# Moving the residual add of four post-norms from VectorE to GpSimd in a two-block transformer kernel

## The chip, the cores and the metric

The kernel runs on one core of a Trainium2 chip. The time is that of one execution on the device in microseconds (us), taken by the host's measurement of the whole program; several runs give a median. One further execution is recorded by the hardware profiler, and all rows below come from it. "PE" is TensorE's matmul stream, "DVE" VectorE, "ACT" ScalarE, "POOL" GpSimd and "SP" SyncE, which only issues transfers here.

## What is computed

The program applies a "first block" and a "second block" of two layers each to a sequence of 512 tokens by 1024 features. Only the ends of the two halves of each layer in the first block matter for this change:

```
def rms_norm(x, g):
    xf = x.astype(jnp.float32)
    y = xf * lax.rsqrt(jnp.mean(xf * xf, axis=-1, keepdims=True) + RMS_EPS)
    return (y * g.astype(jnp.float32)).astype(x.dtype)

for layer in range(DEPTH):                      # first block, DEPTH = 2
    h = rms_norm(x, norm_mix_pre[layer])
    h = dilated_attention_mixer(...) if layer % 2 == 0 else rglru_mixer(...)
    x = x + rms_norm(h, norm_mix_post[layer])   # norms 1 and 3
    h = rms_norm(x, norm_ffn_pre[layer])
    h = conv_ffn(h, ...)
    x = x + rms_norm(h, norm_ffn_post[layer])   # norms 2 and 4
# second block, layer 0 begins with
h = rms_norm_2(x, mix_norm_g[layer])
proj = h @ w_in[layer]
```

So four times a mixer's or feed-forward's output is normed ("post-norm"), added to the residual `x`, and the sum is normed again ("pre-norm") for the next matrix product. The next product of norm 1 and 3 is a feed-forward, that of norm 2 the recurrent mixer, and that of norm 4 the first layer of the second block.

## The kernel before

Activations lie with the features on the partitions: `x`, `y0`, `y1`, `y2`, `h_hi` and `h_lo` are tiles of 128 partitions by 8 chunks by 512 tokens in float32, one chunk (128x512) for 128 features. Matrix products are taken to nearly full float32 accuracy by splitting each operand into a high part (rounded to the matmul's format) and a low part (the rest), and by adding three matmuls: high times high, high times low, low times high. A "unit" is one 128-wide slab of weights: SP loads it into a `raw` buffer, ACT copies it to `w_hi` (line 1353), and the low part `w_lo = raw - w_hi` is taken by GpSimd (line 631 in the attention and recurrent stages, lines 648 and 649 in halves in the second block) or, within the feed-forwards, by DVE (line 2287). PE then multiplies the unit with the eight chunks of the activations (lines 680, 681, 686 and, for the last, 683).

Each engine runs its own instruction stream in program order, with semaphores between the streams. The order is written out by hand, nothing is planned by a scheduler.

The four norms of the first block are the function `norm_pair` of the DVE stream (lines 2111 to 2125) together with `norm_pair` of the ACT stream (lines 1393 to 1398). For every chunk c:

- DVE scales the output: `y = y * gain * rstd` (line 2116, `scalar_tensor_tensor`, raises `res_mid`).
- DVE adds it to the residual: `x = x + y` (line 2120, `tensor_tensor`, raises `x_ready`), one chunk behind the scaling.
- ACT, when `x_ready` says so, writes `h_hi = x * gain` (line 1389) and the square of x into one of two `sq` buffers (line 1381).
- DVE writes `h_lo = x * gain - h_hi` (line 2102), two chunks behind the scaling.

In norms 1, 2 and 3 PE sums the squares over the features itself: `first_unit` (lines 847 to 859) waits per chunk for `h_lo` and the square, issues a matmul of ones with `sq` (line 856) and the three product matmuls of the chunk. In norm 4 (`more=False`) DVE adds up the squares in `ss` (lines 2092 and 2095, one more DVE instruction for each chunk), and PE's first unit belongs to the second block. There ACT, after its last square, loads a table of activation functions (line 2060), splits the first weight unit (line 1353), GpSimd takes its low part (lines 648 and 649), and only then PE can begin.

Of the kernel before, what the change touches and what calls it, by code (L numbers as in the profile page):

```python
# [22 lines left out]
ALU = mybir.AluOpType  # L23
# [5 lines left out]
KC = D // P  # L29
# [38 lines left out]
RING_A, RING_B = 3, 4  # L68
BANKS_A, BANKS_B = 3, 2
AHEAD = 2  # L70
RING_F, AHEAD_F = 6, 5
UNITS_ATTN, UNITS_FFN, UNITS_LRU = HEADS * 9 + KC, FF_BLOCKS * 3 * KC, 3 * KC + 4
# [182 lines left out]
def build_program(nc, t, out):  # L255

    with ExitStack() as ctx:
# [1 line left out]
            [f"raw_A{n}" for n in range(RING_A)] + [f"raw_B{n}" for n in range(RING_B)] +  # L259
            "hi_split unit_ready ffn_ready acc_full acc_freed misc_act misc_dve "  # L260
            "consts_in x_in params_in zeroed t_done x_ready cols_in f_full f_copied f_stored bias_spread bias_in "
            "h_hi h_lo sq_ready ss_ready stat_full rstd_ready res_mid "
            "hi_ready lo_ready v_turned v_hi wide_full wide_freed s_mid nmax_ready exp_done recip p_ready pt_hi pv_full "
            "o_hi o_lo conv_begun conv_mid conv_done gelu_done hid32 hid_hi hid_lo "
            "gate_done xb_ready xb_hi xb_lo lam_act lam_dve r_done a_done w_mid w_done v_done mult_done b_mid hs32 "
# [4 lines left out]
        sems = {n: ctx.enter_context(nc.semaphore(n)) for n in names}  # L270

        def sb(name, shape, dt=F32, c=ctx):
            return c.enter_context(nc.sbuf_tensor("s_" + name, shape, dt))
# [6 lines left out]
        x = sb("x", [P, KC, S])  # L280
        h_hi = sb("h_hi", [P, KC, S], F32R)
        h_lo = sb("h_lo", [P, KC, S], F32R)
        rstd = sb("rstd", [P, S])
# [64 lines left out]
        y0 = sb("y0", [P, KC, S], F32, stage)  # L348
# [3 lines left out]
        y1 = sb("y1", [P, KC, S], F32, stage)  # L352
# [6 lines left out]
        w_hi_a = w_hi + [sb(f"w_hi_f{n}", [P, KC, P], F32R, stage) for n in range(RING_F - RING_A)]  # L359
        w_lo_a = w_lo + [sb(f"w_lo_f{n}", [P, KC, P], F32R, stage) for n in range(RING_F - RING_A)]  # L360
# [11 lines left out]
        y2 = sb("y2", [P, KC, S], F32, stage)  # L372
# [250 lines left out]
        @block.gpsimd  # L623
        def _(pool):
            count = Counts(pool)

            def unit(w_hi_of, w_lo_of):

                pool.wait_ge(sems["hi_split"], count("hi_split"))
                s, w = count.slot(), count.split_slot()  # L630
                pool.tensor_tensor(w_lo_of[w][:], raw_b[s][:], w_hi_of[w][:].bitcast(F32), ALU.subtract).then_inc(sems["unit_ready"], 1)  # L631
                pool.wait_ge(sems["unit_ready"], count("unit_ready"))
                count.units += 1

            for units in (UNITS_ATTN, UNITS_LRU):
                with count.loop(units // RING_A,
                                "hi_split unit_ready") as i:
                    for _ in range(RING_A):
                        unit(w_hi_a, w_lo_a)
                for _ in range(units % RING_A):  # L640
                    unit(w_hi_a, w_lo_a)
                count.units += UNITS_FFN
                count("hi_split", UNITS_FFN)
            def unit_by_halves():

                pool.wait_ge(sems["hi_split"], count("hi_split"))
                s, h = count.slot(), KC // 2
                pool.tensor_tensor(w_lo_b[s][:, 0:h, :], raw_b[s][:, 0:h, :], w_hi_b[s][:, 0:h, :].bitcast(F32), ALU.subtract)  # L648
                pool.tensor_tensor(w_lo_b[s][:, h:, :], raw_b[s][:, h:, :], w_hi_b[s][:, h:, :].bitcast(F32),  # L649
                                   ALU.subtract).then_inc(sems["unit_ready"], 1)  # L650
                pool.wait_ge(sems["unit_ready"], count("unit_ready"))
                count.units += 1

            count.second_ring()
            with count.loop(LAYERS * UNITS_LAYER // RING_B,
                            "hi_split unit_ready") as i:
                for _ in range(RING_B):
                    unit_by_halves()
# [3 lines left out]
        def _(pe):  # L662
# [59 lines left out]
            for c in range(KC):  # L722
                if past := count("x_ready", lag=2):
                    pe.wait_ge(sems["x_ready"], past)
                turn4(bank[c % 2], [x_in[:, j, c * P:(c + 1) * P] for j in range(TT)], "t_done")

            n_dma = sum(copies * (1 + (at % P + rows - 1) // P) for at, rows, _, copies in COLS.values())
            pe.wait_ge(sems["params_in"], count("params_in", 16 * n_dma))
            if past := count("x_ready", 0):
# [612 lines left out]
        def _(act):  # L1342
# [231 lines left out]
            def sigmoids(n):  # L1574
                for dst in (r4, i4):
                    for _, b in tiles(n):
                        output(False)
                        freed()
                        fn(dst[:, b, :], dst[:, b, :], ACT.Sigmoid).then_inc(sems["r_done"], 1)
                        act.wait_ge(sems["r_done"], count("r_done"))  # L1580
# [6 lines left out]
            def decays(n):  # L1587
                nc.scalar.preload_act_table_set("natural_log_exp_and_others")
                for j, b in tiles(n):
                    fn(a4[:, b, :], r4[:, b, :], ACT.Exp, scale=lam(j)).then_inc(sems["a_done"], 1)  # L1590
                    act.wait_ge(sems["a_done"], count("a_done"))
                for _, b in tiles(n):
                    fn(r4[:, b, :], t4[:, b, :], ACT.Ln, scale=-1.0, bias=1.0).then_inc(sems["w_mid"], 1)
                    act.wait_ge(sems["w_mid"], count("w_mid"))
                for _, b in tiles(n):
                    fn(r4[:, b, :], r4[:, b, :], ACT.Exp, scale=-1.0).then_inc(sems["w_done"], 1)
                    act.wait_ge(sems["w_done"], count("w_done"))
# [479 lines left out]
        def _(dve):  # L2077
            count = Counts(dve)
            count.squares = 0
            tt, stt, ts = nc.vector.tensor_tensor, nc.vector.scalar_tensor_tensor, nc.vector.tensor_scalar  # L2080
# [18 lines left out]
            def next_lo(c, gain, add=True):  # L2099

                dve.wait_ge(sems["h_hi"], count("h_hi"))
                stt(h_lo[:, c, :], x[:, c, :], gain(c), h_hi[:, c, :].bitcast(F32), ALU.mult, ALU.subtract).then_inc(sems["h_lo"], 1)
                count("h_lo")
                if add:
                    add_square()
                else:
                    count("sq_ready")
                    count("ss_ready")
                    count.squares += 1

            def norm_pair(y, post, gain, more=True):

                dve.wait_ge(sems["rstd_ready"], count("rstd_ready"))
                for c in range(KC + 2):
                    if c < KC:
                        stt(y[:, c, :], y[:, c, :], post(c), rstd[:], ALU.mult, ALU.mult).then_inc(sems["res_mid"], 1)
                        count("res_mid")
                    if 1 <= c <= KC:
                        dve.wait_ge(sems["res_mid"], count("res_mid", 0, lag=1 if c < KC else 0))
                        tt(x[:, c - 1, :], x[:, c - 1, :], y[:, c - 1, :], ALU.add).then_inc(sems["x_ready"], 1)  # L2120
                        count("x_ready")
                    if c >= 2:
                        next_lo(c - 2, gain, not more)
                if more:
                    dve.wait_ge(sems["rstd_ready"], count("rstd_ready"))
# [176 lines left out]
            count("hi_split", UNITS_ATTN)  # L2302
            project(y0)
            norm_pair(y0, lambda c: col("norm_mix_post", c), lambda c: col("norm_ffn_pre", c))

            def ffn(layer):
# [48 lines left out]
            count.units += UNITS_LRU  # L2355
            count("hi_split", UNITS_LRU)
            norm_pair(y1, lambda c: col("norm_ffn_post", c), lambda c: col("norm_mix_pre", KC + c))

            nc.vector.memset(xpad[:, 0:LRU_CONV - 1], 0.0).then_inc(sems["zeroed"], 1)
# [115 lines left out]
            gated_lo(7)  # L2475
            project(y2)
            norm_pair(y2, lambda c: col("norm_mix_post", KC + c), lambda c: col("norm_ffn_pre", KC + c))
            ffn(1)
            norm_pair(y1, lambda c: col("norm_ffn_post", KC + c), lambda c: col("mix_norm_g_2", c), False)
# [419 lines left out]
```

## Time and profile before

| what | value |
|---|---|
| time, median of 3 runs | 3382.24 us (3378.85 to 3386.6) |
| time of the profiled execution | 3384.51 us |
| its span, first to last instruction | 3382.5 us |
| mean granted TensorE clock | 0.956 of full speed |
| PE busy | 3125.8 us (92%) |
| DVE busy | 1624.0 us (48%) |
| ACT busy | 1448.3 us (43%) |
| POOL busy | 793.0 us (23%) |

PE is busy for nine tenths of the span. The four norms are among the few places where it waits: they lie at 651.8 to 670.9 us, 1081.8 to 1100.8 us, 1289.9 to 1309.0 us and 1720.0 to 1745.5 us. GpSimd does nothing in any of the four. A row of the profile gives busy times of one group of instructions; a row of the timeline gives the start in us, the duration in us, the engine, line and operation, and in brackets how long the engine had been idle before and which instruction ended that.

### The profile page before, as it was taken

The numbers are of one execution on the slowest core, as the hardware profiler recorded it, in microseconds if no ns is written. First come the engines' busy times: TensorE is split into PE (matmuls) and PEld (weight loads), VectorE is DVE, ScalarE is ACT, GpSimd is POOL, SyncE is SP. The second block draws the span as 40 slices with busy tenths as digits, with TensorE's granted clock in tenths as the row PEclk, the third lists the DMA queues.
The fourth block names the chain that finished last, engine by engine and source line by source line (L and its number), as shares of the span: only waits on it lengthen the run. The fifth ranks groups of instructions, "written<-read, shape, count | busy, mean of one in ns | idle before, by whom it ended". The sixth has DMA issues, their size and how long they took to land.

```text
span 3382.5 us, 43848 instructions
## 1 busy us (share of the span) xinstructions
PE 3125.8 (92%) x13613; PEld 2450.7 (72%) x13613; DVE 1624.0 (48%) x2409; ACT 1448.3 (43%) x2123; POOL 793.0 (23%) x528
## 2 busy tenths in 40 slices
PE   6999999899998888999969988699998998889998
PEld 4788887678886666888847757588886775668886
DVE  4454454475665766565647454511124746341113
ACT  3333333443334565333336565433334666442223
POOL 1333323100000330000013212144443220224443
PEclk8999999899999999999979999799999998889999
DMA  8322222133331223333222111033333210213332
GB/s 197 114 75 81 79 67 73 50 112 94 94 93 56 69 75 87 99 94 94 75 81 63 50 52 51 25 95 97 94 93 95 58 58 26 63 49 95 93 93 75
DMA packets 484181, 269.42 MB, mean 80 GB/s; under 512 B 9482, under 2 KB 475474, under 8 KB 483636
## 3 DMA queue, kind: packets, MB, share of 16 engines
q1 hardware_dynamic: 477252, 255.85, 26.7%
q10 hardware_dynamic: 6768, 11.62, 1.0%
q8 instruction: 77, 1.26, 0.2%
q14 instruction: 84, 0.69, 0.1%
HBM read 264.12 MB, written 12.21 MB: 82 GB/s over the span
## 4 chain that ended last, share of the span: by engine, by line
issue 56%; PE 28%; POOL 12%; DVE 1%; ACT 1%; SPq 1%; DMA 0%; POOLq 0%; ACTq 0%; DVEq 0%
PE acc L680 8%; PE acc L681 8%; PE acc L686 7%; POOL s_w_lo L649 5%; POOL s_w_lo L648 5%; POOL s_w_lo L631 2%; PE acc L683 1%; PE wide L707 1%; PE misc L681 0%; PE misc L680 0%; PE misc L686 0%; SPq L522 0%; DMA s_raw<-attn_w_qkv 0%; DVE s_sc L2254 0%; PE wide L680 0%
## 5 line engine op out<-in xcount | busy, mean ns | idle before, releaser
L680 PE MATMUL acc<-s_h_hi,s_w_hi 128*128 128x512 f32 (+1 forms) x2064 | 855.8, 415 | 58.8 <-POOL s_w_lo L649 37.8
L681 PE MATMUL acc<-s_h_lo,s_w_hi 128*128 128x512 f32 (+1 forms) x2064 | 815.5, 395 | 0.0
L686 PE MATMUL acc<-s_h_hi,s_w_lo 128*128 128x512 f32 (+1 forms) x1806 | 713.4, 395 | 0.0
L648 POOL TENSOR_TENSOR s_w_lo<-s_raw,s_w_hi 128x512 fp32r<-128x512 f32 x208 | 268.4, 1291 | 1550.7 <-ACT s_w_hi L1353 1549.6
L1353 ACT ACTIVATE s_w_hi<-s_raw 128x1024 fp32r<-128x1024 f32 x388 | 411.4, 1060 | 387.3 <-DVE s_x L2860 210.9
L680 PEld LDWEIGHTS acc<-s_h_hi,s_w_hi 128*128 128x128 f32 x2064 | 393.3, 191 | 172.4 <-issue 68.9
L631 POOL TENSOR_TENSOR s_w_lo<-s_raw,s_w_hi 128x1024 fp32r<-128x1024 f32 x108 | 261.6, 2422 | 1010.0 <-ACT s_w_hi L1353 1007.3
L681 PEld LDWEIGHTS acc<-s_h_lo,s_w_hi 128*128 128x128 f32 x2064 | 393.6, 191 | 98.0 <-issue 15.7
L686 PEld LDWEIGHTS acc<-s_h_hi,s_w_lo 128*128 128x128 f32 x1806 | 344.2, 191 | 80.2
L680 PE MATMUL acc<-s_hid_hi,s_w_hi 128*128 128x512 f32 x752 | 297.4, 395 | 0.0
L681 PE MATMUL acc<-s_hid_lo,s_w_hi 128*128 128x512 f32 x752 | 297.3, 395 | 0.0
L649 POOL TENSOR_TENSOR s_w_lo<-s_raw,s_w_hi 128x512 fp32r<-128x512 f32 x208 | 271.4, 1305 | 0.0
L686 PE MATMUL acc<-s_hid_hi,s_w_lo 128*128 128x512 f32 x658 | 260.0, 395 | 0.0
L680 PE MATMUL acc<-s_h_hi,s_w_hi_f 128*128 128x512 f32 x432 | 176.1, 408 | 8.5 <-DVE s_w_lo_f L2287 8.5
L2850 DVE SCALAR_TENSOR_TENSOR s_u<-acc,s_rstd 128x512 f32<-128x512 f32 x64 | 44.3, 692 | 269.7 <-PE acc L683 260.4
L681 PE MATMUL acc<-s_h_lo,s_w_hi_f 128*128 128x512 f32 x432 | 172.2, 399 | 0.0
L680 PEld LDWEIGHTS acc<-s_hid_hi,s_w_hi 128*128 128x128 f32 x752 | 141.5, 188 | 33.9
L681 PEld LDWEIGHTS acc<-s_hid_lo,s_w_hi 128*128 128x128 f32 x752 | 141.5, 188 | 33.7
L1533 ACT ACTIVATE s_cv<-s_up,s_cols 128x512 f32<-128x512 f32 x96 | 78.5, 818 | 171.2 <-DVE s_up L2322 166.4
L686 PE MATMUL acc<-s_h_hi,s_w_lo_f 128*128 128x512 f32 x378 | 150.8, 399 | 0.0
L2332 DVE SCALAR_TENSOR_TENSOR s_cv<-s_up,s_cols,s_cv 128x512 f32<-128x512 f32 x192 | 144.1, 750 | 6.1
L686 PEld LDWEIGHTS acc<-s_hid_hi,s_w_lo 128*128 128x128 f32 x658 | 123.8, 188 | 29.6
(402 smaller groups left out, 4978.3 us busy)
## 6 DMA issues: line engine op xcount, KB each, us to landing
s_raw<-w_ff SPq DMA_DIRECT2D x128, 512.0 KB, 4.0
s_raw<-ffn_w_up SPq DMA_DIRECT2D x96, 512.0 KB, 3.9
s_raw<-attn_w_qkv SPq DMA_DIRECT2D x72, 512.0 KB, 3.8
s_raw<-ffn_w_down SPq DMA_DIRECT2D x48, 512.0 KB, 3.9
s_raw<-w_in SPq DMA_DIRECT2D x44, 512.0 KB, 4.1
s_raw<-lru_w_in SPq DMA_DIRECT2D x16, 512.0 KB, 3.9
s_raw<-w_out SPq DMA_DIRECT2D x16, 512.0 KB, 3.9
s_raw<-attn_w_o SPq DMA_DIRECT2D x8, 512.0 KB, 3.9
```

Of the source, the lines that this page charges most:

```text
L631: pool.tensor_tensor(w_lo_of[w][:], raw_b[s][:], w_hi_of[w][:].bitcast(F32), ALU.subtract).then_inc(sems["unit_ready"], 1)
L648: pool.tensor_tensor(w_lo_b[s][:, 0:h, :], raw_b[s][:, 0:h, :], w_hi_b[s][:, 0:h, :].bitcast(F32), ALU.subtract)
L649: pool.tensor_tensor(w_lo_b[s][:, h:, :], raw_b[s][:, h:, :], w_hi_b[s][:, h:, :].bitcast(F32), ALU.subtract).then_inc(sems["unit_ready"], 1)
L680: mm(out, ahi, bhi, start=start, stop=False, **kw)
L681: mm(out, ahi, blo, start=False, stop=False, **kw)
L683: mm(out, alo, bhi, start=False, stop=stop, **kw).then_inc(sems[sem], 1)
L686: mm(out, alo, bhi, start=False, stop=stop, **kw)
L707: nc.tensor.transpose(*args)
L1353: fn((w_hi_a if count.ring == "A" else w_hi_b)[w][:], raw_b[s][:], ACT.Copy).then_inc(sems["hi_split"], 1)
L1533: fn(cv[:, s, :], up[:, s, 2:2 + S], ACT.Identity, bias=cols[:, bass.ds(b * KC + v, 1)], scale=cols[:, bass.ds(b * KC + w, 1)]).then_inc(s ...
L2332: stt(cv[:, s, :], up[:, s, tap:tap + S], cols[:, bass.ds(b * KC + w, 1)], cv[:, s, :], ALU.mult, ALU.add).then_inc(sems[sem], 1)
L2850: stt(u2[:, n % 2, :], o[:], 0.0, rstd[:], ALU.max, ALU.mult).then_inc(sems["acc_freed"], 1)
```

## The change

The residual add leaves DVE's loop. DVE raises `post_done` after each scaling; GpSimd waits for it, adds the chunk (`x = x + y`, one `tensor_tensor` of 128x512 in float32 for each of 4 x 8 chunks) and raises `x_ready`, on which ACT goes on as before. To put the adds in their places, GpSimd's loop over weight units is cut: the adds of norm 1 follow the attention's units, the first two units of the recurrent mixer (`AHEAD` = 2, which are split before norm 2) come ahead of the adds of norm 2, and the adds of norms 3 and 4 follow the mixer's units.

```
@@ in the GpSimd stream
-            for units in (UNITS_ATTN, UNITS_LRU):
-                with count.loop(units // RING_A,
+            def residual(y):
+
+                for c in range(KC):
+                    pool.wait_ge(sems["post_done"], count("post_done"))
+                    pool.tensor_tensor(x[:, c, :], x[:, c, :], y[:, c, :], ALU.add).then_inc(sems["x_ready"], 1)
+
+            def units_of(n):
+                with count.loop(n // RING_A,
                                 "hi_split unit_ready") as i:
                     for _ in range(RING_A):
                         unit(w_hi_a, w_lo_a)
-                for _ in range(units % RING_A):
+                for _ in range(n % RING_A):
                     unit(w_hi_a, w_lo_a)
+
+            def feed_forward_units():
+
                 count.units += UNITS_FFN
                 count("hi_split", UNITS_FFN)
+            units_of(UNITS_ATTN)
+            residual(y0)
+            feed_forward_units()
+            for _ in range(AHEAD):
+                unit(w_hi_a, w_lo_a)
+            residual(y1)
+            units_of(UNITS_LRU - AHEAD)
+            residual(y2)
+            feed_forward_units()
+            residual(y1)
@@ in norm_pair of the DVE stream
                 for c in range(KC + 2):
                     if c < KC:
-                        stt(y[:, c, :], y[:, c, :], post(c), rstd[:], ALU.mult, ALU.mult).then_inc(sems["res_mid"], 1)
-                        count("res_mid")
-                    if 1 <= c <= KC:
-                        dve.wait_ge(sems["res_mid"], count("res_mid", 0, lag=1 if c < KC else 0))
-                        tt(x[:, c - 1, :], x[:, c - 1, :], y[:, c - 1, :], ALU.add).then_inc(sems["x_ready"], 1)
-                        count("x_ready")
+                        stt(y[:, c, :], y[:, c, :], post(c), rstd[:], ALU.mult, ALU.mult).then_inc(sems["post_done"], 1)
+                        count("post_done")
                     if c >= 2:
                         next_lo(c - 2, gain, not more)
```

DVE's stream before, at the start of norm 4 (`s_y` the output being scaled, `s_h_lo` the low part, `s_ss` the sum of squares; lines 2116, 2120, 2102, 2092 and 2095 as above):

```order
L2116 SCALAR_TENSOR_TENSOR s_y<-s_y,s_cols,s_rstd 128x512 x2
L2120 TENSOR_TENSOR s_x<-s_x,s_y 128x512
L2116 SCALAR_TENSOR_TENSOR s_y<-s_y,s_cols,s_rstd 128x512
L2120 TENSOR_TENSOR s_x<-s_x,s_y 128x512
L2102 SCALAR_TENSOR_TENSOR s_h_lo<-s_x,s_cols,s_h_hi 128x512
L2092 COPY s_ss<-s_sq 128x512
L2116 SCALAR_TENSOR_TENSOR s_y<-s_y,s_cols,s_rstd 128x512
L2120 TENSOR_TENSOR s_x<-s_x,s_y 128x512
L2102 SCALAR_TENSOR_TENSOR s_h_lo<-s_x,s_cols,s_h_hi 128x512
L2095 TENSOR_TENSOR s_ss<-s_ss,s_sq 128x512
```

The same stretch of DVE's stream in the changed kernel, where these lines are numbered 2135, 2121, 2111 and 2114:

```order
L2135 SCALAR_TENSOR_TENSOR s_y<-s_y,s_cols,s_rstd 128x512 x3
L2121 SCALAR_TENSOR_TENSOR s_h_lo<-s_x,s_cols,s_h_hi 128x512
L2111 COPY s_ss<-s_sq 128x512
L2135 SCALAR_TENSOR_TENSOR s_y<-s_y,s_cols,s_rstd 128x512
L2121 SCALAR_TENSOR_TENSOR s_h_lo<-s_x,s_cols,s_h_hi 128x512
L2114 TENSOR_TENSOR s_ss<-s_ss,s_sq 128x512
```

The eight adds are gone from it; three scalings now stand ahead of the first low part, and nothing else has changed places. Norms 1 to 3 are the same without the rows of `s_ss`.

GpSimd's stream in the changed kernel, from the last two units of the attention stage to the first unit after norm 2 (before, the rows of line 639 were not there; `waits` names the semaphores):

```order
L631 TENSOR_TENSOR s_w_lo0<-s_raw0,s_w_hi0 128x1024 [waits hi_split]
L631 TENSOR_TENSOR s_w_lo1<-s_raw1,s_w_hi1 128x1024 [waits hi_split,unit_ready]
L639 TENSOR_TENSOR s_x<-s_x,s_y0 128x512 [waits post_done,unit_ready]
L639 TENSOR_TENSOR s_x<-s_x,s_y0 128x512 [waits post_done] x7
L631 TENSOR_TENSOR s_w_lo2<-s_raw2,s_w_hi2 128x1024 [waits hi_split]
L631 TENSOR_TENSOR s_w_lo0<-s_raw0,s_w_hi0 128x1024 [waits hi_split,unit_ready]
L639 TENSOR_TENSOR s_x<-s_x,s_y1 128x512 [waits post_done,unit_ready]
L639 TENSOR_TENSOR s_x<-s_x,s_y1 128x512 [waits post_done] x7
```

Each group of eight adds stands behind the last weight unit that is needed before its norm.

## Rows read from the trace of the kernel before

**Rows 1.** One line's instructions (count, ns min/median/max), and who waited (us, times).

```profile
L2116 DVE SCALAR_TENSOR_TENSOR s_y<-s_y,s_cols,s_rstd x32: 742/746/754, 651.8 to 1734.3; 128x512 f32<-128x512 f32 x32
L2120 DVE TENSOR_TENSOR s_x<-s_x,s_y x32: 680/684/696, 653.2 to 1736.9; 128x512 f32<-128x512 f32 x32
...
  PE misc L856: 20.6, 3
```

**Rows 2.** Timeline of norm 1, DVE and ACT, from its first scaling.

```profile
651.82 1.42 DVE L2116 SCALAR_TENSOR_TENSOR s_y<-s_y,s_cols,s_rstd 128x512 f32<-128x512 f32 x2 [2.56 <-ACT s_rstd L1375]
...
655.02 0.74 DVE L2102 SCALAR_TENSOR_TENSOR s_h_lo<-s_x,s_cols,s_h_hi 128x512 fp32r<-128x512 f32 x1
655.69 0.75 DVE L2116 SCALAR_TENSOR_TENSOR s_y<-s_y,s_cols,s_rstd 128x512 f32<-128x512 f32 x1
...
656.95 0.75 DVE L2102 SCALAR_TENSOR_TENSOR s_h_lo<-s_x,s_cols,s_h_hi 128x512 fp32r<-128x512 f32 x1
...
667.02 0.75 DVE L2102 SCALAR_TENSOR_TENSOR s_h_lo<-s_x,s_cols,s_h_hi 128x512 fp32r<-128x512 f32 x1 [0.34 <-ACT s_h_hi L1389]
...
653.93 0.72 ACT L1389 ACTIVATE s_h_hi<-s_x,s_cols 128x512 fp32r<-128x512 f32 x1 [2.14 <-DVE s_x L2120]
```

**Rows 3.** Timeline of norm 1, PE: chunks 1, 3 and 8, and the end.

```profile
655.98 2.04 PE L856 MATMUL misc<-s_sq,s_square 128*128 128x512 f32 x2 [6.86 <-DVE s_h_lo L2102]
...
661.34 1.02 PE L856 MATMUL misc<-s_sq,s_square 128*128 128x512 f32 x2
...
669.14 1.02 PE L856 MATMUL misc<-s_sq,s_square 128*128 128x512 f32 x2
...
670.47 0.40 PE L683 MATMUL acc<-s_h_hi,s_w_lo 128*128 128x512 f32 x1
```

**Rows 4.** Timeline of norm 4, DVE, ACT and PE.

```profile
1720.04 1.41 DVE L2116 SCALAR_TENSOR_TENSOR s_y<-s_y,s_cols,s_rstd 128x512 f32<-128x512 f32 x2 [4.83 <-ACT s_rstd L1375]
...
1736.88 0.68 DVE L2120 TENSOR_TENSOR s_x<-s_x,s_y 128x512 f32<-128x512 f32 x1
...
1741.65 1.06 ACT L1353 ACTIVATE s_w_hi<-s_raw 128x1024 fp32r<-128x1024 f32 x1 [1.31 <-issue]
...
1745.49 0.79 PE L680 MATMUL acc<-s_h_hi,s_w_hi 128*128 128x512 f32 x1 [28.15 <-POOL s_w_lo L649]
```

**Rows 5.** Timeline of GpSimd alone: two splits back to back, and before norm 2.

```profile
1742.78 1.27 POOL L648 TENSOR_TENSOR s_w_lo<-s_raw,s_w_hi 128x512 fp32r<-128x512 f32 x1 [470.78 <-ACT s_w_hi L1353]
1744.01 1.25 POOL L649 TENSOR_TENSOR s_w_lo<-s_raw,s_w_hi 128x512 fp32r<-128x512 f32 x1
...
1071.84 2.40 POOL L631 TENSOR_TENSOR s_w_lo<-s_raw,s_w_hi 128x1024 fp32r<-128x1024 f32 x1 [12.71 <-ACT s_w_hi L1353]
```

**Rows 6.** Timeline in the second block, DVE and GpSimd at the same time.

```profile
1965.43 1.01 DVE L2684 TENSOR_TENSOR s_tn<-s_tn,s_rope 32x512 f32<-32x512 f32 x1
1966.48 1.67 DVE L2687 TENSOR_TENSOR s_tn<-s_tn,s_cq 32x512 f32<-32x512 f32 x1
...
1964.61 1.29 POOL L649 TENSOR_TENSOR s_w_lo<-s_raw,s_w_hi 128x512 fp32r<-128x512 f32 x1
1966.06 1.54 POOL L648 TENSOR_TENSOR s_w_lo<-s_raw,s_w_hi 128x512 fp32r<-128x512 f32 x1 [0.16 <-POOL s_w_lo L649]
1967.57 1.71 POOL L649 TENSOR_TENSOR s_w_lo<-s_raw,s_w_hi 128x512 fp32r<-128x512 f32 x1
```

**Rows 7.** The same two engines at another place, DVE without waits between.

```profile
2188.15 0.79 DVE L2102 SCALAR_TENSOR_TENSOR s_h_lo<-s_x,s_cols,s_h_hi 128x512 fp32r<-128x512 f32 x1 [0.31 <-ACT s_h_hi L1998]
2188.87 1.76 DVE L2095 TENSOR_TENSOR s_ss<-s_ss,s_sq 128x512 f32<-128x512 f32 x1
...
2188.35 1.73 POOL L649 TENSOR_TENSOR s_w_lo<-s_raw,s_w_hi 128x512 fp32r<-128x512 f32 x1
```

**Rows 8.** Busy us of each engine in a stretch, then granted clock (1.00 is full).

```profile
651.00:659.00 8.00, 3.02 (x5) 1.82 (x6) 7.18 (x12) 4.84 (x8) 0.00 (x0) 0.50 0.27 74
...
2052.00:2060.00 8.00, 5.30 (x26) 3.80 (x26) 7.59 (x17) 6.17 (x11) 0.00 (x0) 1.00 0.01 2
```

More of the change, by code:

```diff
@@ L261, in build_program @@
             "consts_in x_in params_in zeroed t_done x_ready cols_in f_full f_copied f_stored bias_spread bias_in "
-            "h_hi h_lo sq_ready ss_ready stat_full rstd_ready res_mid "
+            "post_done h_hi h_lo sq_ready ss_ready stat_full rstd_ready res_mid "
             "hi_ready lo_ready v_turned v_hi wide_full wide_freed s_mid nmax_ready exp_done recip p_ready pt_hi pv_full "
```

## The prediction

> **What bounds the kernel now.** I read the page's busy shares first: PE is busy for 92% of the span, so time is won or lost where PE waits. The list of who waited for whom names the norms: PE waited 20.6 us in three waits for the low parts of norms 1 to 3 [rows 1], 6.87 us each. The four norms run alike (32 scalings within 742 to 754 ns, 32 adds within 680 to 696 ns [rows 1]), so norm 1 stands for 2 and 3.
>
> Count from the first scaling, at 651.82. DVE issues an instruction some 0.66 us behind the last, a little under its duration (655.02 to 655.69), and its three instructions of a chunk give a rhythm of 1.93 us (655.02 to 656.95) [rows 2]. ACT's first high part starts 2.11 in, the first low part ends 3.94 in, the last one 15.95 in [rows 2]. PE starts 4.16 in, takes 5.36 for its first two chunks and 1.56 for each of the other six, and ends 19.05 in [rows 3]: the last chunk starts at 669.14, though its low part was there at 667.77. So in norms 1 to 3 **PE is the one that ends last**, 1.4 us behind DVE; what counts is when the first low part comes, and whether the others come faster than PE eats them.
>
> Norm 4 is different. DVE has a fourth instruction per chunk (0.60 us more, a rhythm of 2.53), and PE consumes nothing. The last add ends 17.52 in (1737.56); ACT's last high part and square, a table load and the weight split at 1741.65 follow, then GpSimd's low part, and PE at 1745.49 [rows 4]. Here **the last add is on the path**, with nothing beside it.
>
> **The change, part by part.** *The adds leave DVE:* 8 x 0.60 us less to issue per norm. In norms 1 to 3 that alone gives nearly nothing, since PE is behind. *GpSimd takes them:* the trace has no such add on GpSimd; nearest is its subtract of two 128x512 float32 tiles, 1.27 us alone, 1.23 between two starts [rows 5]. Alone, an add would fit into either rhythm. *The queue:* the two weight units ahead of norm 2's adds are over at 1074.24, 7.6 us before its first scaling [rows 5], and in the other norms GpSimd is idle; no unit holds an add back. *Waits:* DVE loses its wait for `res_mid` and gains none; GpSimd's add waits for the scaling, and ACT for the add. The hand-over through a semaphore costs about 0.1 (DVE to ACT, 2.02 to 2.11 in), as before.
>
> *What the two engines do to each other* decides. In the second block [rows 6], DVE's L2687 reads two SBUF tiles and lasts 1.67, where a `tensor_tensor` of the same 512 elements takes 0.68 (the adds [rows 1]); it starts 0.42 after a GpSimd subtract and ends 0.55 after that one's end. The next subtract lasts 1.71 instead of 1.27. The ends of the three GpSimd instructions are 1965.90, 1967.60 and 1969.28: 1.70 and 1.68 apart, where alone they are 1.23. At another place [rows 7] DVE's L2102 and L2095, the very instructions of the norm, run without a wait between them: the subtract that arrives at 2188.35 is let in between, lasting 1.73, and L2095 stands for 1.76. So two-SBUF-input work of DVE and GpSimd's work **exclude each other and take turns**, one instruction each. A turn of both costs 1.69; a further DVE instruction behind it 0.66 (a scaling or low part) or 0.60 (an add). Every DVE instruction of the norms has two SBUF tiles as inputs, except the first sum of norm 4, a copy.
>
> The rule for this is in the Trainium skill, "SBUF — State Buffer", section "Who interferes with whom": a VectorE instruction with two SBUF inputs and a GpSimd instruction that reads SBUF contend for one shared read interface, and whoever has it keeps it for the whole instruction. The rows agree in kind. In size they are milder: whole durations would make a turn 0.75 + 1.27 = 2.02, the rows say 1.69.
>
> *Norms 1 to 3, step by step* (from the first scaling). Scaling 0 ends at 0.74, and scaling 1 is already running; add 0 gets in at 1.3 and ends at 2.55. Scaling 2, add 1, low part 0, add 2 take turns: adds 1 and 2 end at 4.3 and 6.0. ACT's high part 0 runs from 2.7, and low part 0 ends at 4.9 instead of 3.94 because add 1 is in its way. From then on each chunk is an add and a scaling in turn plus a low part: 1.69 + 0.66 = 2.35, **more than the 1.93 before and than PE's 1.56**. Adds 3 to 7: 6.0 + 5 x 2.35 = 17.8. Low part 6 waits for add 7 and ends at 18.6; PE takes chunk 7 of 8 at 18.8 and is through at 18.8 + 2 x 1.56 = 21.9. Against 19.05 that is +2.9 us, of which 0.9 come from the late start and the rest from PE's waits. After the norm everything hangs on PE's last chunk or on the rstd that follows it, so nothing takes it back. Three norms: +8.7.
>
> *Norm 4.* Adds 0 to 2 as above, to 6.0; then a turn and two more DVE instructions for each chunk, 1.69 + 0.66 + 0.60 = 2.95. Add 7 ends at 6.0 + 5 x 2.95 = 20.8 against 17.52: +3.3 us, all on the path.
>
> *Sum:* 8.7 + 3.3 = **+12 us**. The profiled execution, 3384.5 us, would become 3396.5; it is 2.3 us over the median of the runs shown, so the median goes from 3382.2 to **3394**.
>
> *Bounds of the turn.* If GpSimd's add holds the tiles no longer than DVE's own 0.6 suggests for handing over, a turn is as short as 1.6 and the sum about 8 us; at 1.8, the larger end that the durations allow [rows 6, 7], about 16 us. A gain from the unknown price of the add itself is excluded while turns are taken, since even 1.6 + 0.66 is over 1.93. I take 1.69, as it comes from three instructions in a row.
>
> **Rivals.** *A: the adds do not exclude DVE's work* (ending on the other side). Then add 0 runs 0.84 to 2.11, low part 0 no longer stands behind a scaling and an add and ends 0.15 earlier, and PE, bound by itself, ends 0.15 earlier: -0.45 in three norms. In norm 4 DVE's rhythm is 1.93, the last scaling ends at 12.5 and add 7 at 13.9: -3.6. Sum -4.1, 3378 us: no change that a measurement can tell. It decides by whether a turn plus 0.66 lies under 1.93. Both places speak against it [rows 6, 7]; for it only that they show subtracts, not adds.
>
> *B: the interface is held for whole instructions*, as the skill's sentence has it. By the rows as a mechanism: each chunk's turn 2.02 instead of 1.69, 0.33 x 32 = 10.6 us more, 3405. Against it stand the 1.70 and 1.68 [rows 6].
>
> *C: PE's clock does not come up.* PE begins the norm at a granted clock of 0.50, its level of 1.2 GHz, and eats a chunk in some 3.1 us, the third only in 1.56 [rows 3, 8]. If its waits of 0.8 us per chunk kept it at the low level, PE would need 5.1 + 8 x 3.1 = 29.9 instead of 21.9 in each of three norms, 24 us more, 3418. Against it: a stretch where PE was busy for 5.30 of 8 us stayed at 1.00, the level of 2.4 GHz [rows 8], and the first three chunks still run without a gap.
>
> *D: GpSimd starves*, because DVE's stream stays ahead in turn. GpSimd was let in between two instructions that followed one another [rows 7]; and DVE must soon wait for a high part anyway. It gives some 12 to 16 us, inside the range.
>
> That the change doesn't do what it says I leave out: the streams show the adds where they are described.
>
> **How the numbers follow.** Forecast with D 0.84, A 0.09, B 0.03, C 0.04. A measurement of this kernel can tell about 0.2%, 6.8 us. The forecast's own span, 8 to 16 us and 3 us of scatter of a median, is 3387 to 3401, and it holds 8 in 10 alone; A below and C above are left out, B half. Slower by over 0.2%: nearly all of the forecast (0.80, as its low end touches the border), B and C: 0.87. Within 0.2%: the rest and nearly all of A, 0.12. Faster: 0.01.
>
> **What would show it.** Right: GpSimd's adds record about 1.7 us each, not 1.27, and every other scaling or low part of DVE 1.7 to 1.8 instead of 0.75; adds 2.35 apart in norms 1 to 3 and 2.95 in norm 4; the first low part some 0.9 us later after the first scaling; PE's first unit over 21.9 after it instead of 19.05, with waits of 0.8 before chunks 4 to 7; norm 4's add 7 at 20.8. Wrong: adds of 1.3 us beside scalings of 0.75 (A), a granted clock of 0.50 through a whole first unit (C), or a later stretch, say the start of the feed-forward, in which PE waits less than before and gives the loss back.

## The result and the profile after

| | before | after |
|---|---|---|
| median, same chip and session | 3382.96 us (3378.85 to 3388.53, 13 runs) | 3390.77 us (3388.77 to 3393.44, 13 runs) |
| ratio to before | | 1.0023, 95% interval 1.0015 to 1.0032 |
| span of the profiled execution | 3382.5 us | 3388.9 us |
| mean granted TensorE clock | 0.956 | 0.954 |

The change makes the kernel 7.8 us slower (5.1 to 10.8 by the interval). Two more sets of runs of the changed kernel, on the chips and in the sessions of the experiments, gave ratios of 1.0016 (1.0007 to 1.0026) and 1.0020 (1.0011 to 1.0029), so 6 to 8 us in three sets. One further run of the second set took 3587.53 us at a granted clock of 0.821 and is not counted.

First the lines themselves, as in [rows 1]: count, ns min/median/max, and who waited for them (us, times), in the changed kernel.

```profile
L2135 DVE SCALAR_TENSOR_TENSOR s_y<-s_y,s_cols,s_rstd x32: 739/1751/1774, 651.0 to 1747.0; 128x512 f32<-128x512 f32 x32
L639 POOL TENSOR_TENSOR s_x<-s_x,s_y x32: 1637/1707/1727, 651.9 to 1747.8; 128x512 f32<-128x512 f32 x32
...
  PE misc L875: 26.1, 9
```

The median scaling went from 746 to 1751 ns, though nothing about the instruction changed, and GpSimd's adds take 1707. PE's waits for the low parts of norms 1 to 3 rose from 20.6 us in three to 26.1 in nine: it now waits inside the norms too.

The timeline of norm 1 (start, duration, engine, line), DVE, then GpSimd, then PE, answers to [rows 2] and [rows 3]:

```profile
650.96 3.08 DVE L2135 SCALAR_TENSOR_TENSOR s_y<-s_y,s_cols,s_rstd 128x512 f32<-128x512 f32 x3 [2.56 <-ACT s_rstd L1394]
654.34 1.37 DVE L2121 SCALAR_TENSOR_TENSOR s_h_lo<-s_x,s_cols,s_h_hi 128x512 fp32r<-128x512 f32 x1 [0.30 <-ACT s_h_hi L1408]
655.64 1.75 DVE L2135 SCALAR_TENSOR_TENSOR s_y<-s_y,s_cols,s_rstd 128x512 f32<-128x512 f32 x1
657.31 0.74 DVE L2121 SCALAR_TENSOR_TENSOR s_h_lo<-s_x,s_cols,s_h_hi 128x512 fp32r<-128x512 f32 x1
657.97 1.77 DVE L2135 SCALAR_TENSOR_TENSOR s_y<-s_y,s_cols,s_rstd 128x512 f32<-128x512 f32 x1
...
651.86 4.98 POOL L639 TENSOR_TENSOR s_x<-s_x,s_y 128x512 f32<-128x512 f32 x3 [19.62 <-DVE s_y L2135]
657.46 1.72 POOL L639 TENSOR_TENSOR s_x<-s_x,s_y 128x512 f32<-128x512 f32 x1 [0.63 <-DVE s_y L2135]
659.82 1.72 POOL L639 TENSOR_TENSOR s_x<-s_x,s_y 128x512 f32<-128x512 f32 x1 [0.63 <-DVE s_y L2135]
...
666.84 1.71 POOL L639 TENSOR_TENSOR s_x<-s_x,s_y 128x512 f32<-128x512 f32 x1 [0.63 <-DVE s_y L2135]
...
655.92 2.04 PE L875 MATMUL misc<-s_sq,s_square 128*128 128x512 f32 x2 [7.67 <-DVE s_h_lo L2121]
...
665.14 1.12 PE L875 MATMUL misc<-s_sq,s_square 128*128 128x512 f32 x2 [0.51 <-DVE s_h_lo L2121]
...
670.82 1.02 PE L875 MATMUL misc<-s_sq,s_square 128*128 128x512 f32 x2
...
672.13 0.39 PE L702 MATMUL acc<-s_h_hi,s_w_lo 128*128 128x512 f32 x1
```

The adds start 2.36 us apart (657.46 to 659.82), and each scaling is held until the add beside it is through; the low part between them runs in its usual 0.74. The last add ends 17.59 after the first scaling (before 14.20), PE's first unit 21.56 after it (before 19.05).

Norm 4, DVE, GpSimd and PE, against [rows 4]:

```profile
1728.94 3.08 DVE L2135 SCALAR_TENSOR_TENSOR s_y<-s_y,s_cols,s_rstd 128x512 f32<-128x512 f32 x3 [4.54 <-ACT s_rstd L1394]
...
1733.62 1.48 DVE L2111 COPY s_ss<-s_sq 128x512 f32<-128x512 f32 x1
...
1735.69 0.74 DVE L2121 SCALAR_TENSOR_TENSOR s_h_lo<-s_x,s_cols,s_h_hi 128x512 fp32r<-128x512 f32 x1
1736.35 1.74 DVE L2114 TENSOR_TENSOR s_ss<-s_ss,s_sq 128x512 f32<-128x512 f32 x1
...
1735.85 1.70 POOL L639 TENSOR_TENSOR s_x<-s_x,s_y 128x512 f32<-128x512 f32 x1 [1.02 <-DVE s_y L2135]
1738.84 1.70 POOL L639 TENSOR_TENSOR s_x<-s_x,s_y 128x512 f32<-128x512 f32 x1 [1.29 <-DVE s_y L2135]
...
1747.81 1.70 POOL L639 TENSOR_TENSOR s_x<-s_x,s_y 128x512 f32<-128x512 f32 x1 [1.29 <-DVE s_y L2135]
...
1757.44 0.79 PE L699 MATMUL acc<-s_h_hi,s_w_hi 128*128 128x512 f32 x1 [31.19 <-POOL s_w_lo L668]
```

Here the sum of squares is what the add holds (1.74), and the adds are 2.99 apart. The last one ends 20.57 after the first scaling (before 17.52), and PE begins 28.50 after it (before 25.45).

The four norms are thus 2.51, 2.57, 2.46 and 3.05 us longer, **10.6 us together**, in the first profile of the changed kernel, and the last adds of the two others end within 0.02 us of the same places. The time rose by less: 7.8, 6.0 and 6.8 us by the medians of the three sets. Where the other 3 to 5 us went was the question that remained.

### The profile page after: what moved, and what is told of

Its sections match the earlier page's. It is cut to its first block, busy times and chain, and to the rows that moved or that the text cites. A ratio compares the mean times of both kernels' runs of the same rounds, so it can differ in the third digit from the quotient of the medians.

```text
span 3388.9 us, 43845 instructions
## 1 busy us (share of the span) xinstructions
PE 3126.3 (92%) x13613; PEld 2450.0 (72%) x13613; DVE 1637.3 (48%) x2377; ACT 1448.0 (43%) x2123; POOL 847.7 (25%) x560
## 4 chain that ended last, share of the span: by engine, by line
PE 53%; issue 29%; POOL 12%; DVE 3%; ACT 1%; SPq 1%; POOLq 0%; DMA 0%; ACTq 0%; DVEq 0%
PE acc L699 16%; PE acc L700 16%; PE acc L705 14%; POOL s_w_lo L668 5%; POOL s_w_lo L667 5%; PE acc L702 2%; POOL s_w_lo L631 2%; DVE s_y L2135 1%; PE wide L726 1%; DVE s_h_lo L2121 0%; PE misc L700 0%; PE misc L699 0%; PE misc L705 0%; POOL s_x L639 0%; PE wide L699 0%
## 5 line engine op out<-in xcount | busy, mean ns | idle before, releaser
L639 POOL TENSOR_TENSOR s_x<-s_x,s_y 128x512 f32<-128x512 f32 x32 | 54.2, 1703 | 479.1 <-DVE s_y L2135 479.1
```

Of the source, the lines that this page charges most:

```text
L639: pool.tensor_tensor(x[:, c, :], x[:, c, :], y[:, c, :], ALU.add).then_inc(sems["x_ready"], 1)
```

## The experiments

All ratios are to the kernel before, run on the same chip in the same session. An expectation speaks of what was known when it was written.

**What excludes what: the rstd in PSUM.** All adds stay on GpSimd, but ScalarE writes the post-norm's rstd (the reciprocal root of the mean square, by which DVE scales) into a PSUM bank (`wide[0]`, free in these norms), and DVE's scaling reads it there:

```
-                stats()
+                stats(dst=wide[0][:, 0:S])          # the Exp writes there
...
-   stt(y[:, c, :], y[:, c, :], post(c), rstd[:], ALU.mult, ALU.mult)
+   stt(y[:, c, :], y[:, c, :], post(c), wide[0][:, 0:S], ALU.mult, ALU.mult)
```

> All adds are GpSimd's, but ScalarE writes the post-norm's rstd into a PSUM bank, so that VectorE's scaling has one SBUF input and one in PSUM. By the theory that only work with two SBUF inputs excludes GpSimd's: scalings back to 0.75 us beside the adds, low parts (and norm 4's sums) still in turn with them at up to 1.7; in norms 1 to 3 the TensorE's first unit ends 19.0 after the first scaling instead of 21.6; in norm 4 the last add ends at about 19.8 instead of 20.6; together some 8 us less than the changed kernel has in its norms. The rival, that GpSimd's work slows any VectorE work beside it (or that an add lasts 1.7 for a reason of its own): scalings of 1.7 stay, and the time is the changed kernel's.

Measured: 3380.71 us, ratio 0.9990 (0.9981 to 0.9999), 10 us below the changed kernel of the same session. The two lines of this variant, and DVE, GpSimd and PE in norm 1:

```profile
L2136 DVE SCALAR_TENSOR_TENSOR s_y<-s_y,s_cols,wide x32: 733/735/748, 654.2 to 1742.9; 128x512 f32<-128x512 f32 x32
...
L639 POOL TENSOR_TENSOR s_x<-s_x,s_y x32: 1256/1708/1737, 655.1 to 1743.7; 128x512 f32<-128x512 f32 x32
...
654.21 2.06 DVE L2136 SCALAR_TENSOR_TENSOR s_y<-s_y,s_cols,wide 128x512 f32<-128x512 f32 x3 [2.53 <-ACT wide L1394]
657.21 0.92 DVE L2121 SCALAR_TENSOR_TENSOR s_h_lo<-s_x,s_cols,s_h_hi 128x512 fp32r<-128x512 f32 x1 [0.94 <-ACT s_h_hi L1408]
658.06 0.73 DVE L2136 SCALAR_TENSOR_TENSOR s_y<-s_y,s_cols,wide 128x512 f32<-128x512 f32 x1
658.71 1.10 DVE L2121 SCALAR_TENSOR_TENSOR s_h_lo<-s_x,s_cols,s_h_hi 128x512 fp32r<-128x512 f32 x1
...
655.10 9.21 POOL L639 TENSOR_TENSOR s_x<-s_x,s_y 128x512 f32<-128x512 f32 x6 [19.58 <-DVE s_y L2136]
...
672.78 0.40 PE L702 MATMUL acc<-s_h_hi,s_w_lo 128*128 128x512 f32 x1
```

No scaling of the 32 is over 748 ns now, though 20 of them run beside an add for at least part of their time; the first adds, which have scalings alone beside them, take 1263 to 1267 ns. Only low parts and, in norm 4, the sums of squares still take turns with the adds. PE ends 18.97 after the first scaling, the last add of norm 4 at 19.66 (expected 19.0 and 19.8). So it is not GpSimd's work as such that slows these instructions of DVE, but their use of two SBUF tensors beside it: moving one input out of SBUF frees the scaling (a copy within SBUF is a case of its own, see the last section). The Trainium skill, "SBUF — State Buffer", section "Who interferes with whom", says just this of a VectorE instruction with at most one SBUF input; the 735 ns bear it out.

**Norm 4 alone on GpSimd.** In the changed kernel, `on_pool = not more` in DVE's `norm_pair` chooses the old loop for norms 1 to 3, and `residual` is left out of GpSimd's stream three times.

> Only norm 4's adds are GpSimd's; norms 1 to 3 add on VectorE as before. By the theory of turns norm 4's last add ends 20.6 after the first scaling instead of 17.5, norms 1 to 3 end 19.0 after theirs, and the time is 3.0 us over before (3386). By the theory that the second block gives a later start back, the time is that of before, within 1 us, though norm 4 is 3 us longer.

Measured: 3385.95 us, 1.0006 (0.9996 to 1.0015), that is +1.3 us (-1.4 to +5.1). The norms came out as expected: last adds 14.2, 14.2, 14.2 and 20.6 after their first scalings. The time can't tell +3.0 from 0. It is 4.8 us below the changed kernel of the same session, whose norms 1 to 3 are 7.5 us longer.

**The same, with rstd and squares of norm 4 in PSUM**, so that only the low part has two SBUF inputs. In norm 4 ScalarE's squares go to `wide[1]`, from which DVE sums them.

> Norms 1 to 3 as before; in norm 4 the adds are GpSimd's, and both the rstd and the squares that VectorE sums lie in PSUM, so that the low part alone has two SBUF inputs. By the theory of turns each chunk is one turn of add and low part beside which nothing else waits: the last add ends about 14.5 after the first scaling, against 17.5 before and 20.6 in the changed kernel, and the time is 3 us below before (3380). The rival that GpSimd's work slows all of VectorE's gives 20.6 and a time 3 us over before.

Measured: 3377.9 us, 0.9981 (0.9972 to 0.9990). DVE and GpSimd in norm 4:

```profile
1729.80 0.73 DVE L2135 SCALAR_TENSOR_TENSOR s_y<-s_y,s_cols,wide 128x512 f32<-128x512 f32 x1
1730.45 0.74 DVE L2118 SCALAR_TENSOR_TENSOR s_h_lo<-s_x,s_cols,s_h_hi 128x512 fp32r<-128x512 f32 x1
1731.12 0.67 DVE L2111 TENSOR_TENSOR s_ss<-s_ss,wide 128x512 f32<-128x512 f32 x1
...
1730.61 1.71 POOL L639 TENSOR_TENSOR s_x<-s_x,s_y 128x512 f32<-128x512 f32 x1 [0.21 <-DVE s_y L2135]
1732.53 1.71 POOL L639 TENSOR_TENSOR s_x<-s_x,s_y 128x512 f32<-128x512 f32 x1 [0.21 <-DVE s_y L2135]
```

The scalings and the sums are never held here, and of the low parts only the first (0.92) and the seventh (1.16). Else it is the add that waits for the low part's turn (1.71); adds come 1.92 apart, by DVE's three remaining instructions. The last add ends at 14.64 (expected 14.5), 2.9 us earlier than before. **The same move of eight adds costs 3.05 us or gains 2.9, by where two other tensors lie.** The time fell by 6.8 us (3.4 to 9.5), more than the norm explains.

**All adds on GpSimd, all rstds and norm 4's squares in PSUM**, twice:

> All adds are GpSimd's, all post-norm rstds in PSUM, and the squares of norm 4 too. By the theory of turns norms 1 to 3 end as before (TensorE's first unit 19.0 after the first scaling), norm 4's last add at 14.6, and the time is that of the variant with GpSimd's adds in norm 4 alone and the same two tiles in PSUM: 3 to 7 us below before. If instead GpSimd's adds cost norms 1 to 3 something that the first unit's end does not show, it is above that variant by over 2 us.

> The fastest variant (all adds GpSimd's, post-norm rstds and norm 4's squares in PSUM) once more. Its norms are 3 us shorter than before's in sum, and it was 7.6 us faster. If only its norms count, 3 us below before; if something more is gained every time, 6 to 9 below.

Measured: 3375.02 us, 0.9973 (0.9962 to 0.9984), and 3375.16 us, 0.9974 (0.9965 to 0.9984), 7.6 and 7.7 us below before. This is the fastest version. First low parts end 3.9 after the first scaling as before, norm 4's last add at 14.58. Its norms explain 2.9 us, so both times more was gained than they account for.

**Is it the PSUM, not the adds?** All adds on DVE, tensors in PSUM as in the last variant.

> All adds are VectorE's as before, and the rstd of the post-norms and the squares of norm 4 lie in PSUM. It tells whether the two variants that came out below before (-6.8 and -7.6 us) owe it to the adds that left VectorE or to PSUM itself. If to the adds, every norm runs as before (first unit 19.0, norm 4's last add 17.5) and the time is within 1 us of before; if to PSUM, it is 3 to 7 us below.

Measured: 3381.35 us, 0.9999 (0.9990 to 1.0008); norm 4's last add ends at 17.73. PSUM by itself gains nothing that can be measured; by the interval at most 3.4 us.

**Is it GpSimd's rearranged stream?** The changed stream of weight units, without `residual`, all adds on DVE.

> GpSimd's stream is cut and rearranged as in the changed kernel (the first two units of the recurrent mixer written out ahead, its loop shorter), but all adds are VectorE's as before. All four timed variants came out 2 to 6 us under what their norms alone predict (+10.6, +3.05, +2.1, -2.9 against +6.1, +1.3, -4.0, -6.8). If that is a common gain of the rearranged stream, this kernel is 3 to 4 us under before; if it is scatter or the second block's answer to a shift, it is within 1 us of before.

Measured: 3382.71 us, 0.9999 (0.9990 to 1.0008). No gain shows; the interval reaches to 3.4 us below before, so a gain of 3 is just not excluded.

**Does the second block give back any late start?** The kernel before with a pure delay on ScalarE in norm 4, and then with delays spread over the four norms:

```
+                else:
+                    for n in range(14):
+                        fn(y0[:, 0, :], x[:, 0, :], ACT.Square).then_inc(sems["delayed"], 1)
+                        act.wait_ge(sems["delayed"], n + 1)
```

> The kernel before with 14 more squares of 128x512 on ScalarE, one after the other, behind the last square of norm 4, whose results nobody uses; some 0.75 us each, so the second block begins 10.5 us later and all norms run as before. If nothing after norm 4 gives time back, the time is 10.5 us over before (3395). If the second block gives part of any late start back, as 4 to 6 us seemed to be given back behind the changed kernel's norms, it is 5 to 7 over.

Measured: 3393.58 us, 1.0033 (1.0021 to 1.0045). The squares took less than I had taken them for:

```profile
1739.43 9.22 ACT L1401 ACTIVATE s_y<-s_x 128x512 f32<-128x512 f32 x14
```

So the delay was 9.5 us with its wait, and +10.9 us (7.1 to 15.2) were measured: no give-back shows.

> The kernel before with four more squares on ScalarE in each of the four norms, between the logarithm and the exponential of the post-norm's rstd, one after the other, with results that nobody uses; by the row of the 14 squares behind norm 4 (9.22 us, 0.66 each) every norm starts 2.6 us later, 10.6 in all, which is the sum by which the changed kernel's norms are longer and nearly its spread, without GpSimd. If each late start of a stage is lost in full, the time is 10.6 us over before. If losses spread over the norms are partly given back by the clock's answer to a shift (the reading of the changed kernel's 6 to 8 us), it is 6 to 8 over.

Measured: 3392.51 us, 1.0034 (1.0023 to 1.0044), 9.7 us over before by the medians (7.8 to 14.9 by the interval); the changed kernel of the same session, whose expectation was

> The changed kernel a third time, beside the kernel with spread delays on the same chip, since 10.6 and 7 us can only be told apart with more runs. Scatter alone: between 8 and 13 us over before. A real give-back: 6 to 8 again, as in both sets so far, and again 4 to 6 us given back between norm 4 and the end of its profile.

had 3389.66 us, 1.0020 (1.0011 to 1.0029), 6.8 us over by the medians (3.7 to 9.8). Losses that are made without GpSimd stay in full as far as the intervals tell; those of the changed kernel show as 6 to 8 again. The intervals of the two overlap, so the difference rests on three sets of the changed kernel beside two kinds of delay.

**Where it is given back.** Repeats of the changed kernel and of before:

> The changed kernel once more, with a second profile, to tell scatter from cause. The first profile showed norms 1 to 4 longer by 2.5, 2.6, 2.5 and 3.05 us, 10.6 in all, but a time only 6.4 us above the profiled run of before at the end: the difference was 12.4 us at the end of norm 4 and then fell in the second block. Theory 1 (the chip's clock dips fall by chance in each execution): the norms are again longer by 10.6, and the rest of the difference lies elsewhere and has another size, by some us either way. Theory 2 (the second block gives 6 us back whenever it is reached later): the difference falls again by about 6 us at the same places of the second block, and the median stays at 6 to 8 us over before.

> The kernel before once more, for a second profile. All five profiles of changed kernels reach the start of norm 3 some 3.5 us later against the start of norm 2 than the one profile of before, the ones with slow norms 1.6 us later; and at the other end three of them lose 4 to 6 us of their lead between norm 4 and the end. If both come from where the clock's dips fell in the one profile of before, the second profile of before differs from the first by as much at the same places. If they come from the changes, it runs like the first to within 1 us at every norm.

The second profile of before runs like the first after its start: its norms begin 430.21, 208.20 and 430.14 us apart, the first's 430.02, 208.06 and 430.14. From the first rstd of the second block to that of its last feed-forward, the windows of both profiles of before, then of the three of the changed kernel (length, busy us and count of PE, PEld, DVE, ACT, POOL, granted clock, DMA share, GB/s):

```profile
1754.70:3013.67 1258.97, 1146.33 (x5007) 874.52 (x5006) 557.06 (x1012) 627.54 (x1098) 368.34 (x288) 0.94 0.23 64
...
1750.58:3009.97 1259.39, 1145.81 (x5007) 874.12 (x5006) 556.69 (x1012) 627.58 (x1098) 368.35 (x288) 0.94 0.23 64
...
1767.13:3020.77 1253.64, 1140.67 (x5007) 871.67 (x5006) 558.02 (x1012) 627.34 (x1098) 368.47 (x288) 0.94 0.23 65
...
1769.11:3021.87 1252.76, 1140.34 (x5007) 871.69 (x5006) 557.85 (x1012) 627.30 (x1098) 368.52 (x288) 0.94 0.23 65
...
1766.57:3019.73 1253.16, 1142.44 (x5007) 872.53 (x5006) 557.80 (x1012) 627.37 (x1098) 368.52 (x288) 0.94 0.23 64
```

The same 5007 matmuls take 6.0 us less on average (1253.2 against 1259.2), and 4.9 of them are PE's busy time (1141.15 against 1146.07), not its waits. No matmul was taken out, and PE spends less of its busy time at a granted clock of 0.50: summed over the clock records of this window, 123.0 and 122.6 us before, 111.4, 111.9 and 114.8 after. At half the rate each us there does half a us of work, so some 10 us fewer are worth about 5 (an estimate). At one place it can be seen: the same work, in before and, 12 us later, in the changed kernel:

```profile
1934.00:1936.00 2.00, 2.00 (x5) 1.25 (x5) 0.71 (x2) 1.83 (x4) 0.00 (x0) 0.50 0.48 139
1936.00:1938.00 2.00, 2.00 (x4) 0.87 (x4) 0.53 (x2) 1.75 (x4) 0.00 (x0) 0.50 0.41 123
...
1946.00:1948.00 2.00, 2.00 (x8) 0.97 (x7) 0.42 (x1) 1.83 (x4) 0.00 (x0) 1.00 0.15 40
1948.00:1950.00 2.00, 2.00 (x9) 1.51 (x8) 0.56 (x1) 1.83 (x4) 0.00 (x0) 1.00 0.76 226
```

Before, PE goes through it at 0.50, its 1.2 GHz, and does 9 matmuls in 4 us; after, at 1.00, its 2.4 GHz, it does 17. The opposite happens in the recurrent mixer, between the rstd after norm 2 and the one that opens norm 3: both profiles of before, one of the changed kernel, and the kernel with the delay in norm 4, which up to there has the instructions of before.

```profile
1103.53:1289.24 185.71, 158.45 (x639) 122.97 (x637) 127.56 (x141) 110.55 (x138) 65.17 (x26) 0.96 0.26 75
...
1099.33:1285.07 185.74, 158.53 (x639) 123.06 (x637) 127.56 (x141) 110.53 (x139) 65.20 (x26) 0.96 0.26 75
...
1108.05:1295.45 187.40, 160.46 (x639) 123.65 (x637) 127.59 (x141) 110.56 (x138) 65.47 (x26) 0.93 0.26 76
...
1100.39:1289.73 189.34, 162.52 (x639) 125.86 (x637) 127.53 (x141) 110.52 (x138) 65.22 (x26) 0.93 0.26 75
```

The changed kernel loses 1.7 us more there, and the delay kernel 3.6 before anything in it differs. The fastest kernel has both lengths in its two profiles:

```profile
1104.54:1293.91 189.37, 162.50 (x639) 125.73 (x637) 127.57 (x141) 110.53 (x138) 65.42 (x26) 0.93 0.26 75
...
1101.13:1286.87 185.74, 158.53 (x639) 123.07 (x637) 127.54 (x141) 110.56 (x138) 65.46 (x26) 0.96 0.26 75
```

So the clock's share of a stretch changes by some us between executions of the very same kernel. The changed kernel has 187.3 to 187.4 in all three profiles; of the others, all but the spread delays (188.7) lie at 185.7 to 185.8 or at 189.3 to 189.4. Its +1.7 is thus counted against the two profiles of before that there are, not against a fixed time.

For the changed kernel the parts add up to 10.6 + 1.7 - 6.0 = 6.3 us, near the 7.8, 6.0 and 6.8 that the three sets of runs measured. The sum leaves out the start: the first scaling of norm 1 comes at 651.82 and 647.32 us in the two profiles of before, and at 650.96, 653.00 and 650.45 in those of the changed kernel, so the start alone scatters by up to 4.5 us in one kernel.

Whether the 6.0 us have a cause or are chance, the profiles don't settle. The three of the changed kernel agree within 0.9 us. But the fastest kernel's two have 1252.44 and 1256.41 us in the same window, the kernel with norm 4's adds alone on GpSimd 1259.31, the two controls with DVE's adds 1256.39 (PSUM) and 1256.62 (rearranged stream), the delay 1259.71 and the spread delays 1257.18. Over all fourteen profiles the mean is 1254.6 us for the eight with adds on GpSimd and 1258.0 for the six without, and the two groups overlap.

## Why the prediction came out as it did

The direction and the range held: 3390.8 in 3387 to 3401, slower. The forecast of +12 was too high for a measured +7.8.

*The turns* were right step by step. Turn: 1.69 forecast; the first three adds, back to back, take 4.98, 1.66 each, and an add's record is 1.71. Rhythm of the adds: 2.35 forecast, 2.36 measured in norm 1; 2.95 and 2.99 in norm 4. First low part: 4.9 after the first scaling forecast, 4.75 measured. Last add: 17.8 and 17.59; in norm 4, 20.8 and 20.57. The variant with the rstd in PSUM shows that the shared inputs are the cause, since it takes nothing else away. What the prediction had wrong in them is the copy of norm 4, which it set apart from the work with two SBUF inputs: it was held too (1.48). And at a turn of 1.6 its own terms give about 9 us, not the 8 that it took for the low end, which changes the range by 1 us.

*Norms 1 to 3* were sized at +2.9 each and measured +2.5. The start came 0.15 earlier, and the tail was mis-sized: I let PE take chunk 7 at 18.8 and it did at 18.20 (669.16), because add 7 ended 0.2 earlier and low part 6, which DVE had already issued, ended 0.56 behind it (666.69 + 2.42 = 669.11 in the row below), where I had allowed 0.8. The last two chunks then took 3.36 instead of 3.12 (before, too, the last one takes 1.73 to its end, not 1.56), so of these 0.6 us 0.34 were left at the end. Low part 6 is the second of the two in

```profile
666.69 2.42 DVE L2121 SCALAR_TENSOR_TENSOR s_h_lo<-s_x,s_cols,s_h_hi 128x512 fp32r<-128x512 f32 x2
```

The gaps of 0.8 that I forecast before chunks 4 to 7 came before 5 and 6 alone, whose starts are 2.33 and 2.34 behind the chunks ahead of them, against 1.56 of work (the profile's own count is 0.51 and 0.50); PE came to chunk 4 late from its first chunks at the low clock, and to 7 and 8 when the low parts already came faster. That shifts where the waiting shows, not when the norm ends.

*Norm 4* was sized at +3.3 and measured +3.05, all of it on the path, as the start of PE shows (28.50 against 25.45).

*"Nothing takes it back"* is the step that failed, as far as the medians tell: 10.6 us in the norms, 6 to 8 in the time. Both delays show no give-back for what depends on the order of work. What it left out is the clock: I had used the granted clock only for the first unit after a norm, and not asked where the stretches at 0.50 in the rest of the program would fall when the work before them takes another time. In the profiles the changed kernel took 1.7 us more in the recurrent mixer and 6.0 less in the second block, some 5 of them by the clock. It is not the sign that the prediction named, a stretch in which PE waits less: in the second block PE waits 112.6 and 113.6 us before, 113.0, 112.4 and 110.7 after.

Why the changed kernel's low stretches fall so is not settled: neither a later start, nor the rearranged stream, nor PSUM shows it alone. All five kernels with GpSimd's adds came out lower than their norms say, by 2 to 6 us, and the two controls with DVE's adds did not. Singly these gaps are weak. The first set's interval of the changed kernel (5.1 to 10.8) still holds 10.6, that of the kernel with GpSimd's adds in norm 4 alone holds 3.05, and four of the results share one session's median of before, 3384.66, where the other sessions had 3382.7 to 3383.0. Both 7.8 and 10.6 lie in the stated range, so the range does not tell them apart. That is where it stays open.

*The rivals.* A (no exclusion) is refuted by the scalings of 1751 ns, B (whole durations, a turn of 2.02) by turns of 1.66 to 1.71, D (GpSimd starves) by the even spacing of the adds. C (the clock stays low) did not come: the stretch from 661 to 673 us, with PE's waits in it, has

```profile
661.00:673.00 12.00, 10.89 (x34) 5.88 (x33) 8.85 (x8) 6.69 (x10) 5.66 (x4) 1.00 0.01 1
```

a granted clock of 1.00.

## What to carry to other kernels

Before moving elementwise work from VectorE to GpSimd, look at what VectorE does beside it: if its instructions read two SBUF tensors, the two engines take turns, and an engine that was relieved of 8 x 0.60 us comes out slower. Putting one input of the neighbours into a free PSUM bank turned the same move from 7.8 us slower into 7.6 us faster here, of which the norms themselves account for 10.6 and 2.9. And where gains of some us are judged in a kernel bound by TensorE, count the norm or stage itself in the trace; the whole time also moves with where the clock's low stretches fall.

## What the runs showed of the hardware that I had not expected

- A copy is held too, with its single input. DVE's first sum of norm 4 is a `COPY` of 128x512 from SBUF to SBUF, 420 ns in the median before and 1.48 us beside an add (1733.62 above). The prediction took it for the one instruction of the norm that isn't in the way. From PSUM the same copy took 0.68 us beside an add, and 0.68 as well with all adds on DVE, so there it was not held. Before, its row reads:

```profile
L2092 DVE COPY s_ss<-s_sq x12: 414/420/427, 32.0 to 3332.3; 128x512 f32<-128x512 f32 x12
```

  It is faster than a `tensor_tensor` of 684 ns, and the section of the Trainium skill named above says why that matters: a copy from SBUF to SBUF can use both of VectorE's port pairs, one of which GpSimd shares. The 1.48 beside an add within SBUF, and the 0.68 from PSUM, agree with it.
- Which engine's record is the long one is not fixed: in the changed kernel the record of the scaling is the long one, in the variant with two tensors in PSUM the add's is, with DVE at its full pace. A duration alone doesn't tell who is the cause.
- Two executions of one kernel (the fastest) differ by 3.6 us in one stretch of 186 us, with PE's busy time 4.0 us longer over the same 639 matmuls and a granted clock of 0.93 instead of 0.96.
